# Bidirectional RWKV mixer: both directions added in PSUM, and its tail as one stage by row tile

## The reference

```python
def _wkv_step(S, inp):
    r_t, w_t, k_t, v_t, a_t, b_t = inp
    sa = einsum('zbhvk,zbhk->zbhv', S, a_t)
    S = S * w_t[..., None, :] + sa[..., :, None] * b_t[..., None, :] + v_t[..., :, None] * k_t[..., None, :]
    return S, einsum('zbhvk,zbhk->zbhv', S, r_t)
...
    return state, ys[0] + ys[1][:, ::-1]             # z: two directions

def rwkv_out(y, h, xx, r, k_mod, v, mu, ln_g, ln_b, r_k, g1, g2, wo):
    y = layernorm(y, ln_g, ln_b, GN_EPS)             # per head of 64
    bonus = einsum('bthk,zbthk->bth', _heads(r) * r_k, _heads(k_mod))
    y = y + bonus[..., None] * _heads(v)
    gate = sigmoid((h + xx * mu[5]) @ g1) @ g2
    return (y.reshape(bsz, n, d) * gate) @ wo
...
        x = x + gt1 * yl
        hl2 = rmsnorm_2(x, norm2_g[i]) * (1 + sc2) + sh2
        x = x + gt2 * hier_moe(hl2)                  # router: hl2 @ (1024 x 36), top 2 of 32 experts
```

## Time and profile before

| | |
|---|---|
| median of 3 runs | 4362.19 us (4354.28 to 4366.5) |
| the profiled execution | 4359.36 us, span 4357.5 us |
| PE busy | 3588.4 us (82%) |
| DVE busy | 2089.7 us (48%) |
| ACT busy | 1256.0 us (29%) |
| POOL busy | 1399.2 us (32%) |
| scan, its last 13 heads | 3040 to 3560 us |
| join, transposes, projection, norm and router | 3604.4 to 3783.4 us |
| experts | from about 3805 us |

### The profile page before, as it was taken

The page is one execution under the profiler, slowest core; times in us unless marked ns, Lnnn a source line. Parts: engine busy times, 40 slices in busy tenths (PEclk is TensorE's granted clock), DMA queues, the critical chain, the costliest instruction groups (busy, mean ns, idle before and its releaser), DMA issues. The chain is left out here.

```text
span 4357.5 us, 78337 instructions
## 1 busy us (share of the span) xinstructions
PE 3588.4 (82%) x31346; PEld 2541.5 (58%) x31346; DVE 2089.7 (48%) x3296; ACT 1256.0 (29%) x2779; POOL 1399.2 (32%) x1067
## 2 busy tenths in 40 slices
PE   8889998998999998968777758778999991687874
PEld 6667877566777887742222246528989881522221
DVE  4559854448973455630000056428888865500002
ACT  3342223442223223311111122134455541211112
POOL 4444453343443645710000023205445533300001
PEclk9999999999999999979999879898999995798987
DMA  4125443115441224359999943442222214599997
GB/s 126 45 80 181 174 140 98 33 49 174 174 159 61 100 75 144 124 233 420 421 421 421 421 161 131 138 166 60 65 53 67 69 39 137 211 392 420 420 420 297
DMA packets 272891, 819.10 MB, mean 188 GB/s; under 512 B 92456, under 2 KB 99960, under 8 KB 212832
## 3 DMA queue, kind: packets, MB, share of 16 engines
q1 hardware_dynamic: 264112, 786.14, 49.1%
q0 software_dynamic: 7920, 28.84, 1.7%
q10 hardware_dynamic: 576, 0.09, 0.0%
HBM read 738.84 MB, written 76.12 MB: 187 GB/s over the span
## 5 line engine op out<-in xcount | busy, mean ns | idle before, releaser
L2803 POOL DMA_INDIRECT moe0e_xg<-moe_h,moe_first_rows x19 | 18.0, 950 | 593.7 <-DMA moe_first_rows<-moe_table 544.2
L1209 DVE SCALAR_TENSOR_TENSOR f1u_ada<-hT,condition,f1u_ada 128x512 f32<-128x512 f32 x168 | 199.1, 1254 | 0.2 <-DVE f1u_ada L1209 0.2
L2835 PE MATMUL moe0e_p_g<-moe_ring,moe0e_xT 128*64 128x512 f32 x608 | 173.6, 651 | 18.0 <-issue 9.3
L3733 PE MATMUL scan_bank<-scan_T,scan_off 64*64 64x64 f32 x3840 | 160.3, 221 | 32.4 <-issue 27.9
L3469 POOL TENSOR_TENSOR scan_off<-scan_pairs,scan_join 128x256 f32<-128x256 f32 x240 | 185.7, 812 | 0.0
L2803 POOL DMA_INDIRECT moe1e_xg<-moe_h,moe_first_rows x16 | 15.1, 942 | 493.6 <-DMA moe_first_rows<-moe_table 450.1
L359 POOL TENSOR_TENSOR gmi_w_lo<-gmi_rows_w,gmi_w_hi 128x512 fp32r<-128x512 f32 x64 | 120.3, 1881 | 163.1 <-ACT gmi_w_hi L399 163.1
L2835 PE MATMUL moe0e_p_u<-moe_ring,moe0e_xT 128*64 128x512 f32 x608 | 168.4, 634 | 0.0
L359 POOL TENSOR_TENSOR p_w_lo<-p_rows_w,p_w_hi 128x512 fp32r<-128x512 f32 (+3 forms) x88 | 113.7, 1294 | 162.9 <-ACT p_w_hi L399 162.9
L2902 DVE TENSOR_TENSOR moe0e_gated<-moe0e_gate,moe0e_p_u 128x512 f32<-128x512 f32 x19 | 13.1, 688 | 311.0 <-ACT moe0e_gate L2877 311.0
L3733 PEld LDWEIGHTS scan_bank<-scan_T,scan_off 64*64 64x64 f32 x3840 | 137.5, 136 | 40.6 <-issue 33.7
(11 more groups left out here) (749 smaller groups left out, 10500.6 us busy)
## 6 DMA issues: line engine op xcount, KB each, us to landing
moe_ring<-in_moe_w_gu_dram SPq DMA_DIRECT2D x280, 1024.0 KB, 21.9
moe_ring<-in_moe_w_down_dram SPq DMA_DIRECT2D x140, 1024.0 KB, 22.9
hT<-in_ada_w_dram SPq DMA_DIRECT2D x48, 1024.0 KB, 6.6
f0u_w<-in_ffn_w_gate_up_dram SPq DMA_DIRECT2D x22, 1024.0 KB, 4.8
f1u_w<-in_ffn_w_gate_up_dram SPq DMA_DIRECT2D x22, 1024.0 KB, 4.8
gmi_rows_w<-in_ga_w_in_dram SPq DMA_DIRECT2D x64, 256.0 KB, 2.8
gmo_w<-in_ga_w_out_dram SPq DMA_DIRECT2D x64, 256.0 KB, 3.0
p_rows_w<-in_ab_w_in_dram SPq DMA_DIRECT2D x48, 256.0 KB, 2.7
```

Source lines behind the costliest of these rows:

```text
L1209: ins = V.scalar_tensor_tensor(out=acc[:, z, :], in0=src, scalar=cond[:, n * HALF + k, z:z + 1], in1=acc[:, z, :], op0=ALU.mult, op1=ALU.add)
L2803: pool.indirect_dma_start(xg[:], None, H.h, bass.IndirectOffsetOnAxis(rows[:, 0:1], 0)).then_inc(gathered, 16)
L2835: mm = nc.tensor.matmul(p[r, :], xT[:, kd, r], ring[:, s, half, k, g * HID:(g + 1) * HID], start=(kd == 0), stop=(kd == KD - 1), skip_grou ...
L3733: mm = nc.tensor.matmul(out[r], lhsT[r], rhs[r], start=start, stop=stop, skip_group_check=True)
```

## The change

Nothing of the arithmetic's content changes, apart from the order of additions. In the scan, y of both directions is accumulated in one PSUM bank in the tokens' order: the product of step i writes the rows of its own direction's place, so for odd i (`side`) a product that reads the rows `lo` writes the half `hi`. y is copied once per walk into an SBUF tile `rw_y` (128 x 4 x 1024) that lives on, and the bonus is formed in `rw_bonus` in the same order. POOL gets `w_lo` and `add_shift` for each head, ACT gets the rounding of a block of wo (`w_hi`), and SP stores both split parts to DRAM instead of y and bonus. The five stages behind the scan become one, `mixer_finish` (`rwf`), by row tile. The routed rows are waited for without the clearing stores (`cleared` is a semaphore of its own), and the experts' first ring loads are issued in `route`, where the first routed layer issues them already.

```diff
@@ rwkv_scan, SP @@
-                    store(bS, yb, h, s["stored_bonus"])
+                    sp.wait_ge(s["lo_made"], h + 1)
+                    for d, w in zip(wo, (w_hi, w_lo)):
+                        sp.dma_start(block_of(d, h), w[:].bitcast(F32)).then_inc(s["w_stored"], 16)
@@ rwkv_scan, POOL @@
                     if ahead is not None:
                         factors(ahead)
+                    pool.wait_ge(s["hi_made"], h + 1)
+                    nc.gpsimd.tensor_tensor(w_lo[:], w_raw[:], w_hi[:], ALU.subtract).then_inc(s["lo_made"], 1)
+                    if h:
+                        add_shift(h - 1)
@@ rwkv_scan, ACT @@
-                        A(yo[:, n, :], y_psum, ACT.Copy).then_inc(s["y_copied"], 1)
+                    if j == STEPS:
+                        act.wait_ge(s["y_ready"], w + 1)
+                        A(y[:, :, w * HK:w * HK + HK], y_psum.rearrange("p (m c) -> p m c", c=HK), ACT.Copy).then_inc(s["y_copied"], 1)
@@ rwkv_scan, PE @@
+                def side(n):
+                    return (lo, hi)[n % 2]
+
+                def to_rows(i, lhsT, rhs, start=False, stop=False):
+
+                    for r, n in ((lo, i), (hi, lat - 1 - i)):
+                        mm = nc.tensor.matmul(y_psum[side(n), n // 2 * HK:n // 2 * HK + HK], lhsT[r], rhs[r], start=start, stop=stop, skip_group_check=True)
+                    return mm
+
@@ walk_solve @@
-                        mmul(y_psum, rt(w, j), Sm[:], stop=False)
-                        mmul(y_psum, pairs[u][:, j, 3, :], vs[u][:, j, :], start=False, stop=False)
+                        to_rows(i, rt(w, j), Sm[:], start=i == 0)
+                        to_rows(i, pairs[u][:, j, 3, :], vs[u][:, j, :])
@@ walk_share @@
+                    if j >= CSTEPS:
+                        mm = to_rows(j - CSTEPS, pairs[u][:, j, 1, :], SA[:], stop=j - CSTEPS >= NT)
                     if j < STEPS - 1:
                         mmul(ds_psum, bkT[u][:, j, 0, :], SA[:], start=False).then_inc(s["ds_ready"], 1)
-                    if j >= CSTEPS:
-                        mmul(y_psum, pairs[u][:, j, 1, :], SA[:], start=False).then_inc(s["y_ready"], 1)
@@ rwkv @@
-        rwkv_join(nc, "rwj", S, a, yS, bS, gate, o)
-        load_all(nc, "rwl", [(row[:], mods[0, 2 * D:3 * D].partition_broadcast(P))])
-        norm_transpose(nc, "rwt", S, [o[:, t, :] for t in range(NT)], hT, scaled=False)
...
-        project_split(nc, "rwo", hT[:, :, 0:SEQ], SEQ, jobs, aside=make_rows, fetch=R)
+    rwkv_scan(nc, "scan", S, a, kF, rF, sgF, aF, vS, y, bonus, wo)
+    R, H = take_rows()
+    mixer_finish(nc, "rwf", S, a, y, bonus, gate, wo, x_tiles, mods, R, H)
```

More of the change, by code:

```diff
@@ L3340, in rwkv_scan @@
         Sm, X, SA = sb("Sm", [P, HK]), sb("X", [P, HK]), sb("SA", [P, HK])
-        yo, yb = sb("y", [P, lat, HK]), sb("yb", [P, lat, HK])
-        bon = sb("bonus", [P, lat])
+        w_raw, w_hi, w_lo = sb("w_raw", [P, BANK]), sb("w_hi", [P, BANK], F32R), sb("w_lo", [P, BANK], F32R)
+        shift = [sb(f"shift{u}", [P, HK]) for u in range(2)]
+        bon = sb("bonus", [P, NT])
         rk = sb("rk", [P, lat, CH])
@@ L3965, in _ @@
[L3965 to L3973 removed]
+                    if t >= 2:
+                        act.wait_ge(var_made, t - 1)
@@ new lines, in rest_o, with residual @@
+                def rest_o(t):
+                    for h in range(2):
+                        dve.wait_ge(hi_made, 2 * t + h + 1)
+                        V.tensor_tensor(x_lo[t % 2][:, 4 * h:4 * h + 4, :], tr[h][:], x_hi[t % 2][:, 4 * h:4 * h + 4, :], ALU.subtract).then_inc(lo_made, 1)
+                def residual(t):
+                    if t == 0:
+                        dve.wait_ge(row_loaded, 16)
+                    dve.wait_ge(part_done, t + 1)
+                    for h in range(2):
+                        residuals.mark(V.tensor_tensor(bonus[:, t, halves[h]], out[t % 2][h][:], row[:, halves[h]], ALU.mult))
+                    residuals.wait()
+                    V.tensor_tensor(x_tiles[t], x_tiles[t], bonus[:, t, :], ALU.add).then_inc(residual_made, 1)
@@ new lines, in normal, with add_bias @@
+                def normal(t):
+                    if t == 0:
+                        dve.wait_ge(R.made, 2)
+                    dve.wait_ge(rstd_x_made, t + 1)
+                    V.scalar_tensor_tensor(out=y[:, t, :], in0=x_tiles[t], scalar=rstd_x[:, t:t + 1], in1=R.scale[0], op0=ALU.mult, op1=ALU.mult).then_inc(scaled, 1)
+                    dve.wait_ge(scaled, t + 1)
+                    V.tensor_tensor(y[:, t, :], y[:, t, :], R.shift[0], ALU.add).then_inc(xn_made, 1)
+                def add_bias(t):
+                    dve.wait_ge(logit_done, t + 1)
+                    V.tensor_tensor(H.logits[:, t, :], logit_bank, R.bias, ALU.add).then_inc(logits_made, 1)
@@ new lines, in _ @@
+                centre(0)
+                centre(1)
+                spread(0)
+                join(0)
+                centre(2)
+                rest_o(0)
+                spread(1)
+                join(1)
+                centre(3)
+                rest_o(1)
+                residual(0)
+                normal(0)
+                spread(2)
+                join(2)
+                rest_o(2)
+                residual(1)
+                normal(1)
+                add_bias(0)
+                spread(3)
@@ L4004, in rwkv_gates @@
+                join(3)
+                rest_o(3)
+                residual(2)
+                normal(2)
+                add_bias(1)
+                residual(3)
+                normal(3)
+                add_bias(2)
+                add_bias(3)
 def rwkv_gates(nc, name, S, a, hT, xx, c, sgF, aF, gate):
```

359 lines of the change are left out of this document (226 added, 133 removed).

## The result

The changed kernel takes 4307.8 us (median of 4 runs, 4303.5 to 4311.7) against 4361.9 on the same chip: ratio 0.9877, 95% interval 0.986 to 0.9895. Measured again on another chip it took 4312.4 against 4358.8, ratio 0.9901 (0.9883 to 0.9919). It is faster by 1.0 to 1.2%, 46 to 54 us, where 66 were forecast (4296, range 4275 to 4326). The miss of 12 us hides two large errors: the new stage saved more than forecast, and the scan, costed at 2 us, lost over 30.

What follows compares the result with a forecast made beforehand. PE's issue of product pairs bounds the scan's heads; 179.0 us of unoverlapped stages follow, then the experts' DMA stream. 4359.4 - 69.0 - 1.2 + 2 + 2.2 = 4293.4, as median 4296; range 4275 to 4326.

Steps and rivals of the forecast that it cites:

- The stage: New stage between scan and route: 110 us against 179.0, so -69; about 104 at 417 GB/s, 119 at 280.
- steps A to F: New stage's chain by row tile, from the weights' landing to tile 3's tail and logits, ending at 110 us.
- A: New stage, weights: 11.5 MB must land before tile 0's last product; at 350 GB/s those products end at 37.4 us.
- R's row: New stage: POOL's scale row for the router's norm, loads landed at about 41 us, made at 46; tile 0's norm waits.
- The scan: Scan: +1 us for pairs, +1 for POOL, ACT and SP work, +0.8 in the last walk; its end -2 besides.
- So 2.2 us fit in that gap.: Scan heads: POOL's added w_lo (1.50 us) and shift (0.73) fit where POOL had waited 2.71 us for its mask.
- rival 2: Scan: POOL's new work holds DVE, and DVE holds PE; 35 us, giving 4331; chance 0.10.
- heads with PE 94% busy: Sign to look for: scan heads stay as long as before, with PE 94% busy.
- SP's traffic: Scan: 8 MB of y and bonus stores become 8 MB of split weights on a 61 GB/s queue; costs nothing.
- Y ahead of ds: Scan: seven y products precede ds, leaving 0.70 us where 0.65 is needed; 1 us (bounds 0 and 12), last walk +0.8.
- rival 4: Scan: y products crossing halves empty PE's array, 0.34 us at each of 288 changes, 98 us, giving 4394; chance 0.03.
- Route: Route and gather: the rings' first 12 MB issued beside the gather, +2.2 us (0 to 4); expert stream behind as before.

Runs made afterwards that it cites:

- e1: Changed kernel without GpSimd's two new operations per head in the scan (w_lo and the bonus shift): 4305.4 us, ratio 0.9860 to the kernel before.
- e3: Changed kernel with VectorE's bonus products moved right behind the copy of the bonus sums, nothing left out: 4300.5 us, ratio 0.9854 to the kernel before.
- e2: e1's kernel with 14 of 16 weight blocks neither loaded nor stored in the scan: 4287.7 us, ratio 0.9823 to the kernel before.
- e5: Changed kernel with the scan's weight-block loads and stores moved to the middle of a head: 4292.0 us, ratio 0.9843 to the kernel before.
- e4: Changed kernel with y's products always writing their own direction's half, bonus sums still crossed: 4315.5 us, ratio 0.9884 to the kernel before.

## Why the prediction was right, and where it was not

- **The stage** (-69 forecast, -77.7). The steps A to F are all in the trace, in their order. The term that was mis-sized is A's rate: 402 to 420 GB/s and not the middle of 280 and 417. The prediction's own figure for 417 was 104 us; it measures 101.3. R's row was made at 40.9 us (46 forecast), tile 2 joined at 50.2 (55.5), PE stood 9.1 us for it (about 10). The slow rate of the earlier trace rows was the join stage's and didn't carry over. There the DMA engines were busy (0.96) and the rate went to and fro between 216 to 238 and 400 to 447 GB/s; by the order of the issues, the slow parts are the 256 KB loads of 64-row pieces, and the new stage loads 128 rows and 512 KB at a time.
- **The scan** (+2.8 forecast, +34.0). The failed step is "So 2.2 us fit in that gap.", drawn from one wait of GpSimd for its mask. They fit in GpSimd's gap, and GpSimd was not late. But VectorE's bonus products lay beside them and became long, and those were never costed: the prediction does not mention them (one of 128x512, 0.69 us, became two of 64x256, each 0.42 us alone and 1.0 under GpSimd). That is rival 2's mechanism at some two fifths of its price: 12 us of wait in 13 heads, not 35 in 16, shown by e1 and e3. Rival 2 also said against itself that the waits of PE have no line for DVE; that was so before the change and told nothing of after it. The sign that the prediction gave itself, heads with PE 94% busy, came out at 89%. The Trainium skill's rule ("SBUF - State Buffer", section "SBUF: two separate sides") was the right reading here: e1's 0.42 against 1.0 agrees with it.
- **SP's traffic** was costed at "nothing", as bytes on a queue at 61 GB/s. The failed step is that a mean rate says nothing of a burst; the loads of the raw blocks (256 KB a head) were left out besides. The burst stalls PE's own supply once a head, and the half clock that comes with the long stalls adds to it: 12 to 18 us, shown by e2 and e5.
- **Y ahead of ds**: waits for Sm are 1.0 and 0.8 us in 3040 to 3560, 1.9 and 1.7 before; the reserve of 0.70 us against 0.65 was enough. Whether the last walk stays at 1.2 GHz for it is open: every kernel with the new scan did, crossed or not, with and without GpSimd's work. PE was busy 85% and 81% of the spell at 1.2 GHz in two traces of the kernel before, which came back, and 81% and 80% in two of the changed one, which did not. The walk is 3.5 us longer, against 0.8 forecast. No run has the new scan with the old order.
- **Crossed products** (rival 4) cost nothing that a run shows: theirs last 218 ns in the median as before, and e4 without them is not faster. The Trainium skill ("TensorEngine Tiling (Array Packing)", section "Key Properties") says that a change of tile does not drain, and the trace agrees. Beside the new order of the products they gain a little (5.50 us against 5.95 in two steps of the last walk).
- **Route** (+2.2 forecast, -2.3; in the second pair of traces -6.6). The gather is waited for 12.0 us for 7.7 in the earlier trace rows, 4.3 more and over the bound of 4, and the first refill comes 39.9 us behind the route's start for 36.2. But from there to the last group of the ring's loads the stream takes 451.2 us for 457.9, at 426 GB/s for 420.

That the total fell inside the range is luck: the errors of +31 and of -9 and -5 partly cancel. The range's upper end was made of the stage at 119 to 121, the gather at 4 and the order of ds at 12, and none of the three came; these terms add up to 4320 and not to 4326, and the lower ones to 4281 and not to 4275. SP's traffic had no term in it.

## What to carry to other kernels

Where an engine's program is dense and long, place added transfers by time, not only by sum: the same 0.8 MB per head cost 12 us or more in the burst at the head boundary and little in the middle of a head. For an idle piece without a releaser, look at the queue of kind "instruction" in the DMA view. When work is given to GpSimd's free time, list which two-operand VectorE operations lie beside it and what waits for each; a cheap one can sit ahead of the one that PE waits for. In a stage by tile, look for the in-order engine that carries a wait of one tile into the work of the next; exchanging two blocks of one engine's list was worth 8.5 us of 101.
